# One query pass over 256 tokens, with the top-16 lists taken between the queries

## The reference, cut to what matters

```
qh = (h @ w_q).reshape(t, 8, 2, 128)                  # 16 query columns of 128 per token
s = einsum('thcd,hcnd->thcn', qh, sub_keys)           # 16 score lists of 128 per token
s1, i1 = top_k(s[:, :, 0], 16); s2, i2 = top_k(s[:, :, 1], 16)
cand = s1[..., :, None] + s2[..., None, :]            # the best 16 pairs per head are the experts
top_s, pos = top_k(cand.reshape(t, 8, 256), 16); g = softmax(top_s)
pre = einsum('td,thkd->thk', h, u[eidx]); out = einsum('thk,thkd->td', g * gelu(pre), v[eidx])
```

## Time and profile before

| | |
|---|---|
| median of 3 runs | 2004.68 us (2001.94 to 2007.39) |
| profiled execution | 2011.07 us, span 2009.3 us |
| PE busy | 1891.4 us, 94% |
| DVE, ACT, POOL busy | 63%, 23%, 19% |
| read from HBM | 616.92 MB, mean 308 GB/s |

### The profile page before, as it was taken

How to read it: one execution, slowest core, us unless ns; L and a number is a source line. 1 busy time by engine, 2 the same in 40 slices (tenths; PEclk the granted TensorE clock), 3 DMA queues, 4 the chain that set the end, 5 groups by cost and what they waited for, 6 DMA issues and landing times. The chain is left out here.

```text
span 2009.3 us, 32969 instructions
## 1 busy us (share of the span) xinstructions
PE 1891.4 (94%) x12953; PEld 1755.5 (87%) x12953; DVE 1262.6 (63%) x2817; ACT 468.6 (23%) x1660; POOL 377.4 (19%) x320
## 2 busy tenths in 40 slices
PE   7989999999999899999899989999999999899998
PEld 5877779999999889999888566789999999898998
DVE  6359323898898754442399973318897998544441
ACT  3003312323544300000211023013224444100010
POOL 0100000033333312210000630000333333221210
PEclk9989999999999999999999997999999999999999
DMA  7972248899999999999443120269999999999994
GB/s 301 422 272 84 85 171 349 299 413 398 409 414 415 415 413 414 409 414 352 142 144 141 64 94 0 105 247 361 371 403 401 415 415 415 414 414 415 413 403 150
DMA packets 126202, 621.72 MB, mean 309 GB/s; under 512 B 15388, under 2 KB 17596, under 8 KB 83936
## 3 DMA queue, kind: packets, MB, share of 16 engines
q1 hardware_dynamic: 90832, 379.62, 48.9%
q0 software_dynamic: 33104, 238.85, 29.0%
q10 hardware_dynamic: 2112, 1.14, 0.2%
HBM read 616.92 MB, written 2.62 MB: 308 GB/s over the span
## 5 line engine op out<-in xcount | busy, mean ns | idle before, releaser
L1163 PE MATMUL bank<-expert_coef,ring 128*128 128x152 f32 x4096 | 545.3, 294 | 33.8 <-DMA ring<-in_uv 30.3
L1163 PEld LDWEIGHTS bank<-expert_coef,ring 128*128 128x128 f32 x4096 | 531.8, 190 | 46.8 <-DMA ring<-in_uv 41.6
L1090 POOL DMA_INDIRECT expert_rows<-in_uv,pair_index x208 | 302.0, 1452 | 1213.4 <-DVEq L1555 458.2
L1138 PE MATMUL bank<-h,ring 128*128 128x152 f32 x3712 | 502.5, 294 | 10.8 <-DMA ring<-in_ut 10.6
L1138 PEld LDWEIGHTS bank<-h,ring 128*128 128x128 f32 x3712 | 486.3, 190 | 14.8 <-DMA ring<-in_ut 14.3
L1402 DVE CUSTOM_DVE_ANT_0 expert_rows<-expert_rows,h_tokens 128x1024 f32<-128x1024 f32 x192 | 234.3, 1220 | 170.6 <-DMA expert_rows<-in_uv,pair_index 170.4
L1410 DVE SCALAR_TENSOR_TENSOR pair_sum<-expert_rows,pair_coef,pair_sum 128x1024 f32<-128x1024 f32 x192 | 245.9, 1281 | 51.1 <-ACT pair_coef L1286 49.1
L1284 ACT ACTIVATE pair_act<-pair_dot 128x1 f32<-128x1 f32 x208 | 42.2, 203 | 593.9 <-DVE pair_dot L1402 593.8
L1105 PE MATMUL bank<-h,ring 128*128 128x128 f32 x1024 | 120.0, 282 | 6.1 <-ACT h L1293 3.8
L1105 PEld LDWEIGHTS bank<-h,ring 128*128 128x128 f32 x1024 | 119.4, 198 | 7.0 <-issue 7.0
L1270 ACT ACTIVATE work<-work,choice 128x128 f32<-128x128 f32 x304 | 96.9, 406 | 0.0
(11 more groups left out here) (395 smaller groups left out, 2053.6 us busy)
## 6 DMA issues: line engine op xcount, KB each, us to landing
ring<-in_uv SPq DMA_DIRECT2D x256, 512.0 KB, 14.7
ring<-in_ut SPq DMA_DIRECT2D x232, 512.0 KB, 13.3
ring<-in_dense SPq DMA_DIRECT2D x96, 1024.0 KB, 4.9
ada<-in_ada POOLq DMA_DIRECT2D x16, 1024.0 KB, 17.4
expert_coef<-in_ut SPq DMA_DIRECT2D x24, 512.0 KB, 8.2
ada<-in_ada SPq DMA_DIRECT2D x8, 1024.0 KB, 23.1
expert_rows<-in_uv,pair_index POOLq DMA_INDIRECT x208, 9.9
bias_rows<-proj_t POOLq DMA_DIRECT2D x1, 1536.0 KB, 6.5
```

The source lines that it names most:

```text
L1090: pool.indirect_dma_start(rows[:, p % BUFFERS, :], None, table, bass.IndirectOffsetOnAxis(pindex[:, p:p + 1], 0))\
L1138: ins = nc.tensor.matmul(k.bank[e % 4][:, 0:DENSE], w[:, kk, :], k.h[:, kk, FRONT:TOK], start=kk == 0, stop=kk == KD - 1)
L1163: ins = nc.tensor.matmul(down_bank(i), w[:, i * P:(i + 1) * P], A[:, e, :], start=e == 0 and i % 3 == 0, stop=e == NB - 1, skip_group_chec ...
```

## The change

One pass of 16 query tiles over all 256 tokens; the first tile is still taken half by half, since the halves are normalised one after the other. Scores of four lists for 128 tokens, `score(n)`, follow after each fourth query tile. DVE takes the 16 best of each of these (`lists(n)`) as they come, for both halves, and only then runs `select(0)` and `select(1)`, which no longer contain the lists. The keys no longer pass through the ring but are loaded once into a row buffer, with a semaphore of their own. Groups start after up 37; ten pairs instead of 18 are laid into `select(1)`; the constants that place pairs, exps, choices, early tiles and late gathers are moved.

```diff
-GATES_FROM = 54
-EARLY_PAIRS = 18
-EARLY_AFTER = tuple(9 + 5 * p // 2 for p in range(EARLY_PAIRS))
-EXP_AFTER = (5, 38)
-CHOICE_AFTER = (20, 55)
-SHARED_LISTED = 22
+GATES_FROM = 37
+EARLY_PAIRS = 10
+EARLY_AFTER = tuple(14 + 23 * p // 10 for p in range(EARLY_PAIRS))
+EXP_AFTER = (5, 23)
+CHOICE_AFTER = (12, 40)
+SHARED_LISTED = 13
-AHEAD_UPS = (6, 12, 17, 21, 24, 27, 30, 33, 36, 39, 42, 45)
+AHEAD_UPS = (4, 11, 15, 18, 20, 22, 24, 26, 28, 30, 32, 34)
...
-    for name, chunks in (... ("wq1", 8), ("keys1", 1), ("wq1", 8), ("keys1", 1),
+    for name, chunks in (... ("keys1", 1), ("wq1", 8),      # keys get a place, no ring load
...
+                sp.dma_start(rows[:, 2, :], k.args["dense"][DENSE_AT["keys" + layer], :, :]).then_inc(k.keys_dma, 16)
                 def load_ahead(c):
-                    if c < AHEAD:
-                        sp.dma_start(ahead_tile(c), ...)
+                    for i in range(2 * c, min(2 * c + 2, AHEAD)):
+                        sp.dma_start(ahead_tile(i), ...)
...
-                        pool.wait_ge(k.w_used.sem, k.w_used.at(13 * (p - late - BUFFERS) // 5))
+                        pool.wait_ge(k.w_used.sem, k.w_used.at(14 * (p - late - BUFFERS) // 5))
+                    if p == 2:
+                        pool.wait_ge(k.scored.sem, k.scored.at(8))
...
-                for tt in range(TT):
-                    for c in range(NC2):
-                        query(tt, c)
-                    score(tt)
+                for c in range(NC2):
+                    query(c)                               # 256 columns
+                    if c == 4:
+                        pe.wait_ge(k.keys_dma, 16 * int(layer))
+                    if c % 4 == 0 and c:
+                        for n in range(c // 2 - 2, c // 2):
+                            score(n)
+                for n in range(6, 8):
+                    score(n)
...
+                def lists(n):
+                    q, tt = n // TT, n % TT
+                    cs = range(4 * q, 4 * q + 4)
+                    dve.wait_ge(k.keyed.sem, k.keyed.at(n + 1))
+                    for c in cs:
+                        ch(nc.vector.max(best[:, tt, c, 0:8], s[:, tt, c, :]))
+                    ch.wait()
...                                                        # max_index, match_replace, max, max_index
-                dve.wait_ge(k.keyed.sem, k.keyed.at(4))
+                for n in range(8):
+                    lists(n)
                 select(0)
...
-                dve.wait_ge(k.keyed.sem, k.keyed.at(8))
                 dve.wait_ge(k.copied.sem, k.copied.at(2))
                 select(1)
```

More of the change, by code:

```diff
@@ L111, in plan @@
             at = DENSE_AT.setdefault(name, NDENSE)
-            for c in range(chunks):
+            for c in range(chunks if name[:4] != "keys" else 0):
                 LOADS.append(("dense", at + c, unit, 2))
@@ L990, in peer_layer @@
         index = sb("expert_index", [P, TT, P], I32)
-        best_i = sb("best_index", [P, NC2, PK], U32)
+        best_i = sb("best_index", [P, TT, NC2, PK], U32)
         pos = sb("top_pos", [P, PH, PK], U32)
         whole = sb("picked_int", [P, P], I32)
+        keys = rows[:, 2, :].rearrange("p (c n) -> p c n", n=NKEYS)
         replica = rows[:, BUFFERS - 1, 0:D].rearrange("p (k t) -> p k t", k=KD)
@@ L1062, in _ @@
             def _(sp):
+                sp.dma_start(rows[:, 2, :], k.args["dense"][DENSE_AT["keys" + layer], :, :]).then_inc(k.keys_dma, 16)
                 def load_ahead(c):
-                    if c < AHEAD:
[L1065 to L1069, removed]
+                    for i in range(2 * c, min(2 * c + 2, AHEAD)):
+                        sp.dma_start(ahead_tile(i), k.args["ut" + layer][AHEAD_UPS[i], :, :]).then_inc(k.ahead_loaded[i], 16)
+                refill(k, sp, PASS + NR + NB, None,
+                       [(k.tile_ready, 2 * c + 2) for c in range(PH)]
                        + [(k.pre, e + 1) for e in range(NB) if e not in AHEAD_UPS]
@@ L1095, in _, with query @@
             def _(pe):
-                def query(tt, c):
+                def query(c):
                     if c % 2 == 0:
[L1099 to L1106, removed]
-                    ins.then_inc(k.tile_ready.sem, 1)
@@ L1109, in score @@
[L1109 to L1119, removed]
@@ L1121, in _ @@
-                for tt in range(TT):
-                    for c in range(NC2):
-                        query(tt, c)
-                    score(tt)
+                        arrived(k, pe, c // 2)
+                    w = chunk(k, c // 2).rearrange("p (k n) -> p k n", k=KD)
+                    pe.wait_ge(k.act_emptied.sem, k.act_emptied.at(c - 3))
+                    for cols in (slice(0, P), slice(P, TOK)) if c == 0 else (slice(0, TOK),):
+                        for kk in range(KD):
+                            if c == 0:
+                                pe.wait_ge(normed.sem, normed.at(cols.start // P * KD + kk + 1))
+                            ins = nc.tensor.matmul(k.bank[c % 4][:, cols], w[:, kk, (c % 2) * P:(c % 2 + 1) * P],
+                                                   k.h[:, kk, cols], start=kk == 0, stop=kk == KD - 1)
@@ new lines, in query, with score @@
+                    ins.then_inc(k.tile_ready.sem, 1)
+                def score(n):
+                    q, tt = n // TT, n % TT
+                    pe.wait_ge(k.act_emptied.sem, k.act_emptied.at(4 * q + 4))
+                    pe.wait_ge(k.keyed.sem, k.keyed.at(n - 3))
+                    for c in range(4 * q, 4 * q + 4):
+                        ins = nc.tensor.matmul(k.bank[4 + n % 4][:, (c % 4) * P:(c % 4 + 1) * P],
+                                               qt[:, c, tt * P:(tt + 1) * P], keys[:, c, :], start=True, stop=True)
+                    ins.then_inc(k.scored.sem, 1)
@@ L1293, in _ @@
                         nc.scalar.activation(h, h, ACT.Identity, bias=shift[:, kk:kk + 1]).then_inc(normed.sem, 1)
[L1294 to L1299, removed]
+                for c in range(NC2):
+                    act.wait_ge(k.tile_ready.sem, k.tile_ready.at(c + 1))
+                    nc.scalar.activation(qt[:, c, :], k.bank[c % 4][:, 0:TOK], ACT.Copy).then_inc(k.act_emptied.sem, 1)
+                    if c % 4 == 0 and c:
+                        for n in range(c // 2 - 2, c // 2):
+                            scores(n)
+                for n in range(6, 8):
+                    scores(n)
                 act.wait_ge(normed.sem, normed.at(KD))
@@ L1445, in select @@
[L1445 to L1455, removed]
```

54 lines of the change are left out of this document (28 added, 26 removed).

## The result

The changed kernel took **2043.36 us** (median of 4 runs, 2040.80 to 2049.72) against 2003.64 of the kernel before on the same chip: a ratio of 1.020, 95% interval 1.0171 to 1.0230, about 40 us slower. 2031 was forecast, with 2007 to 2048 as the range. The profiled execution of the changed kernel has a span of 2047.9 us, 38.6 more than before; layer 1 makes 17 of them and layer 2 makes 22.

What follows compares the result with a forecast made beforehand. PE was nearly always busy, its ups narrowly paced by DMA at about 414 GB/s. Stage sums gave +28 us, DMA alone +24; +26 was taken, giving 2031 us, range 2007 to 2048.

Steps and rivals of the forecast that it cites:

- Queries: Query stage with one wide pass: 65.0 us against 66.2, so -1.2 us in layer 2 and -2.3 in layer 1.
- The rival of cheap wide passes: Query stage: wide passes cost far less per column than narrow ones, 23 us a layer less, 1985 us; chance 0.01.
- The lists and the first gather: Behind the queries: four lists take 4.8 us; first gather 39.2 us after up 0's start (E); PE stands 8.3 us.
- the rival by which DVE is done in time: At `choice(0)`: DVE is done when PE comes, 28.7 us after up 0's start; 2005 to 2014 us; chance 0.12.
- Group 0: First group in the ups of layer 2: starts 96.5 us after up 0's start (E), with 13 gathers out.
- From group 0 to the downs: Rest of the ups: 246 us of DMA, 239 with ring tiles; ups end 22 us later, downs 6 us shorter.
- It is worse: After group 0 DMA runs at 402 GB/s instead of 414 and the ring is empty: 2059 us; chance 0.08.
- the first sum: Both layers by stages: -1.2 + 22 - 6 = +14.8 us in layer 2, +13.7 in layer 1, together +28.
- This is the core of the change: 20 us later against up 0: Start of the ups: `select(0)` stands wholly behind the queries, so the first gather leaves 20 us later.
- The second way, +24 by DMA from the first gather: Whole layer by DMA alone: 618 us from up 0's start against 604, +14 a layer, +24 for both with the queries.
- so 16 us are lost there: PE up to group 0 loses 16 us: 8.3 at `choice(0)`, the rest at pairs waiting for ScalarE and group 0.
- Rival, DMA not at its ceiling: Only PE's order counts; waits for ring tiles, 19 us a layer, vanish: some 1993 us, faster; chance 0.1.

Runs made afterwards that it cites:

- half after: The changed kernel with gathers of half a row from the fifth gather on: 1977.93 us, ratio 0.9867 to the kernel before.
- Places: The changed kernel with the places of waits set later (choice 0 after up 17, groups from up 58) and 18 early pairs again: 2010.75 us, ratio 1.0028.
- gates 37: The kernel before, with groups from up 37, ten early pairs, and the changed kernel's early tiles and late pacing: 2047.41 us, ratio 1.0203.
- quarters: The changed kernel with two narrow query passes, first choice found under the second pass, 18 early pairs, groups from up 48: 2003.02 us, ratio 0.9987.
- before, early 10: The kernel before with ten early pairs instead of 18, later pairs at five for seven ups: 2050.32 us, ratio 1.0231.
- half before: The kernel before with gathers of half a row from the fifth on: 1942.96 us, ratio 0.9693.
- after, early 18: The changed kernel with 18 early pairs instead of ten, all ahead of groups that still start from up 37: 2052.59 us, ratio 1.0235.
- quarters 24: The kernel quarters with 24 early pairs instead of 18 and groups from up 54 instead of 48: 2016.48 us, ratio 1.0060 to the kernel before.
- quarters paced: quarters 24 with slower gathers: five pairs per nine gated ups, one late gather per 3.4 downs: 1987.09 us, ratio 0.9917 to the kernel before.

## Why the prediction was right, and where not

**Queries: right.** Layer 2's stage takes 65.0 us, as worked out; 64 wide passes take 13.98 us, 218 ns each, about two narrow ones. The rival of cheap wide passes is out.

**The lists and the first gather: right.** 5.1 us for four lists (1365.18 to 1370.27 in DVE's timeline), not 4.8; the first gather at E+40.0, not E+39.2; the wait at `choice(0)` 8.9 us, not 8.3. With that wait the rival by which DVE is done in time is out.

**Group 0: right.** E+96.1 against E+96.5, 13 gathers out, as counted.

**From group 0 to the downs: right in kind, mis-sized.** The step that failed is "I take 239, bounds 236 and 246": the 7 us that ring tiles were to give back. It took 245.6 us in layer 2 and 243.5 in layer 1: the plain sum of the DMA work, in effect. By the bytes, 245.6 us at 409 GB/s are 100.5 MB, and 52 gathers and 90 tiles are 101.7. So the ring, with what was on its way at group 0, gave some 1.3 MB, 3 us of the 7 that I counted on, and the engines lost these 3 us again by moving 409 GB/s in place of 414. That is a mild form of the rival "It is worse" (402 GB/s and an empty ring). The lower rate begins right behind group 0, here in the changed kernel and then in the kernel before:

```profile
1505.00:1545.00 40.00, 39.55 (x298) 39.07 (x299) 31.06 (x53) 17.60 (x77) 13.56 (x9) 0.96 0.96 377
```

```profile
1511.00:1551.00 40.00, 39.95 (x314) 39.62 (x315) 30.23 (x53) 20.14 (x87) 12.83 (x9) 1.00 1.00 397
```

Why the ring gave no more, and why the rate was lower, was not settled. One reason may lie in PE's own need, for which I took 222 us: half after, with no wait for tiles, takes 230.5 there (326.7 - 96.2), so the two limits lie 15 us apart and not 24. The ups so end 28.1 us later in layer 2 and 23.0 in layer 1, not 22; the downs are shorter by 5.1 and 3.2, not 6. With the queries (-1.1 and -2.7) that is 21.9 and 17.1, and 39 in all, against the 28 of the first sum.

**"This is the core of the change: 20 us later against up 0": wrong as the main cause.** Places has the same first gather at E+40 and loses 7 us; gates 37 has it at E+19.4 and loses 44. Nor does a first gather at E+3 gain anything (quarters). What costs is that the gates begin at up 37 behind only ten early pairs, 21 us ahead of the old place, before DVE is done and with nine gathers fewer out there (five fewer at the same time, E+117.6).

**The second way, +24 by DMA from the first gather, agreed with the first sum by chance.** It says that the layer is as late as its first gather. By it gates 37 should have lost next to nothing, and quarters should have won some 16 us a layer.

**One limit or two.** I let PE's standing vanish under the transfers ("so 16 us are lost there", and then a sum by DMA alone). Tried alone, each limit gives a loss of about that size: transfers 45 us (before, early 10, which is shorter of gathers than the changed kernel, so that 45 is probably more than the changed kernel's own share), PE's standing and clock 35 (half after against half before). They overlap in the changed kernel, so 39 come out and not 80. In layer 2 the ups lose 19.8 us by PE's side; what whole rows in place of half rows add to the ups grows from 6.7 to 15.0 us (313.6 - 306.9 and 341.7 - 326.7), 8.3 more, about as much as the listed waits for tiles there (4.1 to 12.0).

**Rival, DMA not at its ceiling: out.** The changed kernel's ups moved 409 GB/s, not 439, and the waits for the ring did not vanish; no run moved more than 415 from group 0 to down 0. The Trainium skill ("DMA: Bandwidth & Descriptors", Where 436 GB/s comes from) has 435 GB/s for the fabric; what these runs reach there is about 5% less.

## What to carry to other kernels

Where two chains are both nearly full, ask of each what it would give with the other taken away (smaller transfers, or fewer of them at the start); here a loss showed up twice and was paid about once, and removing the shortage of gathers alone (after, early 18) bought nothing. An event that starts earlier is worth only what can follow it: count the transfers that are out at one fixed time in both kernels rather than when the first one leaves. A stream that shares a full DMA with the tiles of the main loop should be spread so that both together ask for a little less than the ceiling: the slower paces alone took quarters 24 from 2016 to 1987 us.

## What the runs showed of the hardware

PE's waits have a tail: after 8.9 us of standing 32 passes took 5.44 us in place of 4.30 (granted clock 0.78), and in half after the lower clock behind two waits cost some 3.7 us of layer 2's ups, beside 14.3 us more of idle time. And DMA engines that are as good as full do not always move the same: from group 0 to down 0 it was 402 GB/s in gates 37 (share 1.00) and in before, early 10 (0.99), 409 in after (1.01) and 414 in quarters paced (1.02). What sets that is open.
